# Second mixer of a three-part network: probabilities and values as rounded high and low parts, their product in three passes

## The chip, the core and the metric

The kernel runs on one core of one Trainium2 chip. A core has a matrix engine (TensorE, PE in the profile; its weight loads are PEld), a vector engine (VectorE, DVE), an activation engine (ScalarE, ACT), a general engine (GpSimd, POOL) and a queue engine (SyncE, SP). The engines run beside each other, each takes its own instructions in their order, and they wait for each other by semaphores. The working memory (SBUF) has 128 partitions; TensorE writes into eight banks of 128x512 float32 numbers (PSUM). The metric is the device time of one execution in microseconds (us).

## The reference

A sequence of 512 rows of width 1024 goes through two layers of feed-forward parts and mixers and one hybrid layer. The change is in the mixer of the second layer, eight heads of differential attention:

```python
q = rms_norm(q.reshape(B, S, DIFF_HEADS, 2, DIFF_DH), qk_norm_g[0]) * (DIFF_DH ** -0.5)
k = rms_norm(k.reshape(B, S, DIFF_HEADS, 2, DIFF_DH), qk_norm_g[1])
p1 = jax.nn.softmax(jnp.einsum('bhqd,bhkd->bhqk', q1b, k1) + bias, axis=-1)
p2 = jax.nn.softmax(jnp.einsum('bhqd,bhkd->bhqk', q2b, k2) + bias, axis=-1)
return jnp.einsum('bhqk,bhkv->bhqv', p1 - lam * p2, vh)
...
out = rms_norm(out, subln_g) * (1.0 - lam_init)
return out.reshape(B, S, DIFF_V).astype(h.dtype) @ w_out
```

The last einsum of the attention is the product that the change touches: for each head 512 queries, 512 keys, 128 columns of values.

## The kernel before

Seven stages follow each other: ffn 0, gla (first mixer), ffn 1, ffn 2, diff (second mixer), ffn 3, hybrid. Weights arrive in panels by SyncE's queue. For each unit of 128 columns ScalarE writes a rounded high part (whi, type float32r) and VectorE the rest as a low part (wlo); TensorE then makes each product of a weight and an activation as three passes of rounded operands: high by high, high by low, low by high (rows, L1989).

In the second mixer the order of everything is one list, diff_steps (L231), and each engine's program walks through it and does its own part of each step. Head h has four query tiles n = 4h to 4h+3. The steps:

- half: four of the eight row tiles of one projection (k, q or v of one head), 12 passes on TensorE. With the second half VectorE subtracts a coming weight unit (w_lo) and multiplies the result out of PSUM (L1725 for q and k, L1720 for v).
- ss, rs, qk, hi, lo: norm of q and k. TensorE sums the squares, ScalarE takes the root, VectorE scales, ScalarE copies the rounded high parts (seven copies of half tiles: dif_k, dif_q), VectorE subtracts for the low parts (four, L1746).
- attend n: TensorE makes two score tiles of two passes each; VectorE adds the bias and takes the maximum (L1758, "the two maxima"); ScalarE takes the exponential.
- comb n: VectorE scales and joins the two tiles into the probabilities (L1787 to L1793).
- turn n: TensorE transposes the four 128x128 blocks of the probabilities into bank 5 (L1986), ScalarE copies the bank to DPT, shown as dif_pt.
- vT h: TensorE transposes the values into bank 6, ScalarE copies them to DV, shown as dif_v.
- pv h: TensorE multiplies DV and DPT, four plain float32 products (L2387), into bank 7.
- oss, o, y: norm of the head's output; begin and more: parts of the output projection, begun while the last head is still going.

In the middle of the stage the list of one pass of its loop (h = 2 to 5) is this; h = 1 begins at half q, and h = 6 ends at half v:

```
half k0, vT h, attend n, comb n-1, o h-2, half k1, turn n-2, half q0,
attend n+1, comb n, turn n-1, half q1, attend n+2, comb n+1, pv h-1, ss h+1,
half v0, rs, qk, hi h+1, turn n, attend n+3, comb n+2, half v1, lo h+1,
oss h-1, turn n+1
```

Turn n waited for d_pt, the copy of turn n-1, because both use bank 5. The product pv waited for the copies of its head's values and of its four turns. ScalarE's order is that of the list too: the copy of turn n comes after hi h+1. All matmuls stand under L1982, all transposes under L1986, and all of ScalarE's instructions under L771 or L772, the lines of the helpers.

Of the kernel before, what the change touches and what calls it, by code (L numbers as in the profile page):

```python
# [9 lines left out]
ALU = mybir.AluOpType  # L10
# [41 lines left out]
NCOLS = _n  # L52
STAGE = 21792

# [347 lines left out]
d_hi_q d_hi_k d_lo_q d_lo_k d_v d_vT d_vrow  # L402
d_score d_max d_exp d_comb d_turn d_pt d_pv d_osq d_oss d_y d_yhi d_ylo
gs h_z h_hi h_conv0 h_conv h_gmm h_gates h_ri h_ix h_tanh h_a h_ln h_m h_sqrt h_one h_b h_scan
# [5 lines left out]
def build(nc, a):  # L410
    with ExitStack() as ctx:
# [74 lines left out]
        with ExitStack() as mem:  # L486
            def t_(name, shape, dt=F32):
                return sb("dif_" + name, shape, dt, mem)

            O = t_("y", [128, 8, S])  # L490
            bt = [t_(f"bias{i}", [128, 896]) for i in range(2)]
            qb = [t_(f"qb{i}", [128, S]) for i in range(2)]
            dsq = [t_(f"sq{i}", [128, S]) for i in range(2)]
            drq = [t_(f"rq{i}", [128, S]) for i in range(2)]
            dparts = [[t_(f"{n}{i}", [128, S], F32R) for n in ("q0", "q1", "k0", "k1", "kl0", "kl1")] for i in range(2)]
            dvt = t_("vt", [128, S])
            DV = [t_(f"v{i}", [128, 4, 128]) for i in range(2)]
            dpb = [[t_(f"p{i}{j}", [128, S]) for j in range(2)] for i in range(3)]
            DPT = t_("pt", [128, 4, S])
            dst = [t_(f"st{i}", [128, 8]) for i in range(3)]  # L500
# [812 lines left out]
        def dve_program(e):  # L1313
# [390 lines left out]
            def diff():  # L1704
                u = first["diff"]
                zero_halves(dparts)
                for s in DS:
                    if s[0] == "half":
                        _, tag, h, half = s
# [54 lines left out]
                    elif s[0] == "o":  # L1764
                        h = s[1]
                        w.wait_ge(sem["lnb"], rsqrt_done(("d_o", h)))
                        e.scalar_tensor_tensor(out=O[:, h, :], in0=psum[DIF_PV][:, :], scalar=lam[:, 7:8], in1=sqs[:, :],
                                               op0=ALU.mult, op1=ALU.mult).then_inc(sem["d_y"], 1)
                    elif s[0] == "y":
                        n = s[1]  # L1770
                        w.wait_ge(sem["d_yhi"], n + 1)
                        e.tensor_tensor(xl[:, n, :], O[:, n, :], xh[:, n, :].bitcast(F32),
                                        ALU.subtract).then_inc(sem["d_ylo"], 1)
                    elif s[0] == "begin" and s[1]:
                        w_lo(u)

            def zero_halves(parts):
# [200 lines left out]
        def pe_program(e):  # L1978
# [332 lines left out]
            def diff_misc_free(key):  # L2311
# [5 lines left out]
                elif key[0] == "vT":  # L2317
                    w.wait_ge(sem["d_vrow"], key[1] + 1)
                else:
                    w.wait_ge(sem["lnb"], ln_done(("q", key[1])))  # L2320

            def diff():
                u = first["diff"]
                misc, in_free, got = None, [], {}
                for s in DS:
# [48 lines left out]
                    elif s[0] == "turn":  # L2374
                        n = s[1]
                        w.wait_ge(sem["d_comb"], 4 * n + 4)
                        if n:
                            w.wait_ge(sem["d_pt"], n)
                        turned(DIF_TURN, dpb[n % 3][0], 4, sem["d_turn"])
                    elif s[0] == "pv":  # L2380
                        h = s[1]
                        w.wait_ge(sem["d_vrow"], h + 1)
                        w.wait_ge(sem["d_pt"], 4 * h + 4)
                        if h:
                            w.wait_ge(sem["d_y"], h)
                        for c in range(4):
                            ins = mm(psum[DIF_PV][:, :], DV[h % 2][:, c, :], DPT[:, c, :], c == 0, c == 3)  # L2387
                        ins.then_inc(sem["d_pv"], 1)
# [21 lines left out]
            def out_bank_free(m):  # L2410
# [7 lines left out]
                elif m == 5:  # L2418
                    w.wait_ge(sem["d_pt"], 32)
                elif m == 6:  # L2420
# [345 lines left out]
```

## Time and profile before

| | |
|---|---|
| median of 3 runs | 2163.85 us (2163.83 to 2165.5) |
| profiled execution | 2163.63 us, of which the span is 2161.8 |
| busy, share of the span | TensorE 99%, weight loads 85%, VectorE 78%, ScalarE 54%, GpSimd 12% |
| chain that ended last | TensorE 91%, VectorE 4%, ScalarE 2% |
| product of the second mixer | 64 records from 1365.8 to 1547.1 us |

Busy shares are means over all stages. What one stage waits for is read from the stage itself: in the rows in order of time, a bracket gives the idle time of an engine ahead of an instruction and what released it. The records of matmuls overlap, so their distance from start to start is what each costs, not their length.

### The profile page before, as it was taken

How to read it: one execution, taken by the hardware profiler on the slowest of the kernel's cores; microseconds unless marked ns; L12 is line 12 of the kernel's file. 1: busy time of each engine (PE TensorE's matmuls, PEld its weight loads, DVE VectorE, ACT ScalarE, POOL GpSimd, SP SyncE). 2: the span in 40 equal slices, each digit the busy share in tenths (PEclk: the TensorE clock that was granted, in tenths of full speed). 3: DMA queues.
4: the chain of work that ended last, by engine and by line, in shares of the span. 5: the costliest groups of instructions: out<-in, count | busy, mean ns of one | idle time of the engine just before them, and what ended most of it. 6: DMA issues, size and time to landing. Idle time of an engine off the chain costs nothing.

```text
span 2161.8 us, 33546 instructions
## 1 busy us (share of the span) xinstructions
PE 2144.5 (99%) x13412; PEld 1835.3 (85%) x13412; DVE 1680.9 (78%) x2546; ACT 1176.7 (54%) x1922; POOL 253.0 (12%) x187
## 2 busy tenths in 40 slices
PE   9999999999999999999999999999999999999999
PEld 6989897777779898989899997777789898977777
DVE  8789697988678796888787787777688886966873
ACT  6536264667556263546355356777555362638672
POOL 3000004000040000040010112000130000030000
PEclk9999999999999999999999999999999999999999
DMA  7454535131135555354554542222135545332211
GB/s 214 123 136 99 151 94 161 40 98 60 46 89 141 124 137 151 84 162 125 176 129 127 122 126 92 77 75 95 50 79 150 137 100 150 98 131 74 79 59 39
DMA packets 249451, 237.75 MB, mean 110 GB/s; under 512 B 4984, under 2 KB 245240, under 8 KB 249296
## 3 DMA queue, kind: packets, MB, share of 16 engines
q1 hardware_dynamic: 208336, 210.25, 30.3%
q0 software_dynamic: 40752, 25.11, 8.7%
q8 instruction: 107, 1.75, 0.3%
q14 instruction: 48, 0.39, 0.1%
q10 hardware_dynamic: 208, 0.24, 0.0%
HBM read 213.79 MB, written 6.32 MB: 102 GB/s over the span
## 4 chain that ended last, share of the span: by engine, by line
PE 91%; DVE 4%; ACT 2%; issue 1%; DMA 0%; SPq 0%; ACTq 0%; DVEq 0%
PE ps L1982 90%; PE ps L1986 1%; DVE sb_wlo L1334 1%; DMA sb_raw<-ffn_w_gu 0%; ACT sb_whi L771 0%; DVE sb_gla_ek L1689 0%; DVE sb_gla_eq L1692 0%; ACT sb_hyb_th L771 0%; ACT sb_lnb L771 0%; DVE sb_gla_cf L1681 0%; DVE sb_gla_xb L1684 0%; DVE sb_gla_d L1669 0%; SPq L737 0%; DVE sb_rb L1965 0%; ACT sb_xh L771 0%
## 5 line engine op out<-in xcount | busy, mean ns | idle before, releaser
L1982 PE MATMUL ps<-sb_xh,sb_whi 128*128 128x512 f32 (+1 forms) x1812 | 625.4, 345 | 3.6 <-issue 1.8
L1982 PE MATMUL ps<-sb_xl,sb_whi 128*128 128x512 f32 (+1 forms) x1812 | 608.8, 337 | 0.1
L1982 PE MATMUL ps<-sb_xh,sb_wlo 128*128 128x512 f32 (+1 forms) x1812 | 606.7, 337 | 0.0
L771 ACT ACTIVATE sb_whi<-sb_raw 128x1024 fp32r<-128x1024 f32 (+1 forms) x368 | 379.9, 1037 | 376.6 <-PE ps L1982 359.8
L1982 PEld LDWEIGHTS ps<-sb_xh,sb_whi 128*128 128x128 f32 x1812 | 344.0, 190 | 56.8 <-issue 20.4
L1982 PEld LDWEIGHTS ps<-sb_xl,sb_whi 128*128 128x128 f32 x1812 | 344.2, 190 | 39.3 <-DVE sb_xl L1354 3.3
L1982 PEld LDWEIGHTS ps<-sb_xh,sb_wlo 128*128 128x128 f32 x1812 | 343.9, 190 | 37.1
L1982 PE MATMUL ps<-sb_ffn_tl,sb_whi 128*128 128x256 f32 x1200 | 339.6, 283 | 0.0
L1982 PE MATMUL ps<-sb_ffn_th,sb_whi 128*128 128x256 f32 x1200 | 339.6, 283 | 0.0
L1982 PE MATMUL ps<-sb_ffn_th,sb_wlo 128*128 128x256 f32 x1200 | 339.6, 283 | 0.0
L1334 DVE TENSOR_TENSOR sb_wlo<-sb_raw,sb_whi 128x1024 fp32r<-128x1024 f32 (+1 forms) x218 | 275.6, 1271 | 49.1 <-ACT sb_whi L771 48.6
L1982 PE MATMUL ps<-sb_ffn_ah,sb_whi 128*128 128x512 f32 x704 | 275.4, 391 | 0.0
L1982 PE MATMUL ps<-sb_ffn_ah,sb_wlo 128*128 128x512 f32 x704 | 274.1, 389 | 0.0
L1982 PE MATMUL ps<-sb_ffn_al,sb_whi 128*128 128x512 f32 x704 | 274.1, 389 | 0.0
L1982 PEld LDWEIGHTS ps<-sb_ffn_tl,sb_whi 128*128 128x128 f32 x1200 | 230.4, 192 | 0.0
L1982 PEld LDWEIGHTS ps<-sb_ffn_th,sb_wlo 128*128 128x128 f32 x1200 | 230.4, 192 | 0.0
L1982 PEld LDWEIGHTS ps<-sb_ffn_th,sb_whi 128*128 128x128 f32 x1200 | 230.4, 192 | 0.0
L2600 POOL DMA_DIRECT2D sb_raw<-sb_raw x75 | 96.4, 1350 | 989.5 <-DMA sb_raw<-ffn_w_gu 736.2
L1327 DVE TENSOR_TENSOR sb_wlo<-sb_raw,sb_whi 128x1024 fp32r<-128x1024 f32 x150 | 182.7, 1218 | 2.4 <-ACT sb_whi L771 2.4
L771 ACT ACTIVATE sb_whi<-sb_ffn_sums 128x1024 fp32r<-128x1024 f32 (+1 forms) x150 | 125.7, 841 | 83.4 <-DVE sb_ffn_sums L1349 64.5
L1982 PEld LDWEIGHTS ps<-sb_ffn_ah,sb_wlo 128*128 128x128 f32 x704 | 132.1, 188 | 27.9
L1982 PEld LDWEIGHTS ps<-sb_ffn_ah,sb_whi 128*128 128x128 f32 x704 | 132.2, 188 | 26.9
(293 smaller groups left out, 2919.9 us busy)
## 6 DMA issues: line engine op xcount, KB each, us to landing
sb_raw<-ffn_w_gu SPq DMA_DIRECT2D x86, 1024.0 KB, 5.8
sb_raw<-ffn_w_down SPq DMA_DIRECT2D x32, 1024.0 KB, 5.1
sb_raw<-sb_raw POOLq DMA_DIRECT2D x75, 256.0 KB, 4.2
sb_raw<-w_ada SPq DMA_DIRECT2D x12, 1024.0 KB, 7.6
sb_raw<-ffn_w_down SPq DMA_DIRECT2D x16, 768.0 KB, 5.6
sb_raw<-gla_w_in SPq DMA_DIRECT2D x12, 1024.0 KB, 5.5
sb_raw<-diff_w_in SPq DMA_DIRECT2D x12, 1024.0 KB, 5.1
sb_raw<-w_in SPq DMA_DIRECT2D x10, 1024.0 KB, 5.1
```

The lines of the kernel that those rows point to most:

```text
L771: return e.activation(out, in_, func, bias=bias, scale=scale)
L1327: e.tensor_tensor(lo, fast_source(u), hi.bitcast(F32), ALU.subtract).then_inc(sem["w_lo"], 1)
L1334: e.tensor_tensor(lo, raw[panel % NRAW][:, 0:nk, off:off + 128], hi.bitcast(F32), ALU.subtract).then_inc(sem["w_lo"], 1)
L1982: return e.matmul(out, lhsT, rhs, start=start, stop=stop, skip_group_check=skip)
L1986: ins = e.transpose(psum[bank][:, c * 128:(c + 1) * 128], src[:, c * 128:(c + 1) * 128], ident)
L2600: e.dma_start(raw[up % NRAW][:, 0:4, off:off + 128], raw[gate % NRAW][:, 0:4, off:off + 128], accum_op=ALU.add).then_inc(sem[f"s_pre{i % 2 ...
```

## The change

The probabilities and the values of the second mixer are kept as two rounded parts. ScalarE's copies out of banks 5 and 6 now write the rounded high part (type float32r), and VectorE subtracts it from the same bank for the low part (new tiles DPTL and DVL). The product of a head becomes 12 passes: for each of four tiles high by high, high by low and low by high. The next turn, the next use of bank 6 after a vT, and the product now wait for the subtraction (d_ptl, d_vlo). VectorE does a subtraction after its next step that has work for it, or when the next turn or vT comes in the list. The first half of a projection has no VectorE work and is skipped in this. The two new tiles take 12 KB per partition; the stages' memory grows by that, and the build reserves less for dynamic DMAs.

```diff
-STAGE = 21792
+STAGE = 24864
...
-            DV = [t_(f"v{i}", [128, 4, 128]) for i in range(2)]
+            DV, DVL = ([t_(f"{n}{i}", [128, 4, 128], F32R) for i in range(2)] for n in ("v", "vl"))
...
-            DPT = t_("pt", [128, 4, S])
+            DPT, DPTL = t_("pt", [128, 4, S], F32R), t_("ptl", [128, 4, S], F32R)
...
             def diff():
                 u = first["diff"]
                 zero_halves(dparts)
+                turned_last = None
                 for s in DS:
+                    if s[0] in ("turn", "vT"):
+                        if turned_last is not None:
+                            low_of_turned(*turned_last)
+                        turned_last = s
+                        if s == ("turn", 31):
+                            low_of_turned(*turned_last)
+                            turned_last = None
+                        continue
                     if s[0] == "half":
                         _, tag, h, half = s
                         if not half:
                             continue
...
                     elif s[0] == "begin" and s[1]:
                         w_lo(u)
+                    else:
+                        continue
+                    if turned_last is not None:
+                        low_of_turned(*turned_last)
+                        turned_last = None
+
+            def low_of_turned(kind, n):
+
+                if kind == "turn":
+                    w.wait_ge(sem["d_pt"], n + 1)
+                    if n >= 4:
+                        w.wait_ge(sem["d_pv"], n // 4)
+                    out = slice(n % 4 * 128, n % 4 * 128 + 128)
+                    e.tensor_tensor(DPTL[:, :, out], psum[DIF_TURN][:, :].rearrange("p (c q) -> p c q", q=128),
+                                    DPT[:, :, out].bitcast(F32), ALU.subtract).then_inc(sem["d_ptl"], 1)
+                else:
+                    w.wait_ge(sem["d_vrow"], n + 1)
+                    if n >= 2:
+                        w.wait_ge(sem["d_pv"], n - 1)
+                    e.tensor_tensor(DVL[n % 2][:, :, :], psum[DIF_MISC][:, :].rearrange("p (s c) -> p s c", c=128),
+                                    DV[n % 2][:, :, :].bitcast(F32), ALU.subtract).then_inc(sem["d_vlo"], 1)
...
                 elif key[0] == "vT":
-                    w.wait_ge(sem["d_vrow"], key[1] + 1)
+                    w.wait_ge(sem["d_vlo"], key[1] + 1)
...
                         w.wait_ge(sem["d_comb"], 4 * n + 4)
                         if n:
-                            w.wait_ge(sem["d_pt"], n)
+                            w.wait_ge(sem["d_ptl"], n)
                         turned(DIF_TURN, dpb[n % 3][0], 4, sem["d_turn"])
                     elif s[0] == "pv":
                         h = s[1]
-                        w.wait_ge(sem["d_vrow"], h + 1)
-                        w.wait_ge(sem["d_pt"], 4 * h + 4)
+                        w.wait_ge(sem["d_vlo"], h + 1)
+                        w.wait_ge(sem["d_ptl"], 4 * h + 4)
                         if h:
                             w.wait_ge(sem["d_y"], h)
                         for c in range(4):
-                            ins = mm(psum[DIF_PV][:, :], DV[h % 2][:, c, :], DPT[:, c, :], c == 0, c == 3)
+                            mm(psum[DIF_PV][:, :], DV[h % 2][:, c, :], DPT[:, c, :], c == 0, False)
+                            mm(psum[DIF_PV][:, :], DV[h % 2][:, c, :], DPTL[:, c, :], False, False)
+                            ins = mm(psum[DIF_PV][:, :], DVL[h % 2][:, c, :], DPT[:, c, :], False, c == 3)
...
-    nc = bacc.Bacc("TRN2", target_bir_lowering=False, num_devices=1)
+    nc = bacc.Bacc("TRN2", target_bir_lowering=False, num_devices=1, dynamic_dma_scratch_size=4096)
```

## Rows read from the trace of the kernel before

**Rows 1.** The page: busy time by engine; the chain that ended last, by engine.
```profile
PE 2144.5 (99%) x13412; PEld 1835.3 (85%) x13412; DVE 1680.9 (78%) x2546; ACT 1176.7 (54%) x1922; POOL 253.0 (12%) x187
...
PE 91%; DVE 4%; ACT 2%; issue 1%; DMA 0%; SPq 0%; ACTq 0%; DVEq 0%
```

**Rows 2.** Groups by form, 1300 to 1570 us: busy, mean ns, idle before.
```profile
L1982 PE MATMUL ps<-sb_dif_pt,sb_dif_v 128*128 128x512 f32 x64 | 28.8, 592 | 0.0
...
L1725 DVE TENSOR_TENSOR sb_dif_qb<-ps,sb_rb 128x512 f32<-128x512 f32 x16 | 10.9, 683 | 1.0 <-ACT sb_rb L771 1.0
```

**Rows 3.** Order of time, TensorE around pv 2: start, length, engine, instruction.
```profile
1420.72 0.39 PE L1982 MATMUL ps<-sb_dif_k,sb_dif_q 128*128 128x512 f32 x1
...
1421.63 3.59 PE L1982 MATMUL ps<-sb_dif_pt,sb_dif_v 128*128 128x512 f32 x8
1425.15 1.09 PE L1982 MATMUL ps<-sb_dif_sq,sb_cst 64*64 64x512 f32 x8
```

**Rows 4.** Order of time, around attend 13 and turn 11.
```profile
1416.79 0.57 ACT L771 ACTIVATE sb_dif_pt<-ps 128x512 f32<-128x512 f32 x1
...
1417.25 0.69 DVE L1758 CUSTOM_DVE_ANT_0 sb_dif_p<-ps,sb_dif_bias 128x512 f32<-128x512 f32 x1 [1.69 <-PE ps L1982]
...
1417.51 0.63 PE L1986 MATMUL ps<-sb_cst,sb_dif_p 128*128 128x128 f32 x4
...
1418.48 0.16 DVE L1787 RECIPROCAL sb_dif_st<-sb_dif_st 128x2 f32<-128x2 f32 x1
```

**Rows 5.** Order of time, end of the half projection of q ahead of pv 2.
```profile
1420.49 0.39 PE L1982 MATMUL ps<-sb_xh,sb_wlo 128*128 128x512 f32 x1
...
1421.07 0.68 DVE L1725 TENSOR_TENSOR sb_dif_qb<-ps,sb_rb 128x512 f32<-128x512 f32 x1
```

**Rows 6.** Order of time, from attend 15 to attend 16.
```profile
1431.38 0.16 DVE L1787 RECIPROCAL sb_dif_st<-sb_dif_st 128x2 f32<-128x2 f32 x1
...
1432.83 1.22 DVE L1334 TENSOR_TENSOR sb_wlo<-sb_raw,sb_whi 128x1024 fp32r<-128x1024 f32 x1
...
1433.25 0.60 ACT L771 ACTIVATE sb_dif_pt<-ps 128x512 f32<-128x512 f32 x1
...
1436.00 1.40 DVE L1746 TENSOR_TENSOR sb_dif_q<-sb_dif_qb,sb_dif_q 64x512 fp32r<-64x512 f32 x2
...
1437.59 0.48 PE L1982 MATMUL ps<-sb_dif_k,sb_dif_q 128*128 128x512 f32 x1
```

**Rows 7.** Order of time, from attend 27 to attend 28.
```profile
1515.21 1.40 DVE L1746 TENSOR_TENSOR sb_dif_kl<-sb_dif_qb,sb_dif_k 64x512 fp32r<-64x512 f32 x2
...
1516.65 1.40 DVE L1746 TENSOR_TENSOR sb_dif_q<-sb_dif_qb,sb_dif_q 64x512 fp32r<-64x512 f32 x2
1517.08 0.60 ACT L771 ACTIVATE sb_dif_pt<-ps 128x512 f32<-128x512 f32 x1
...
1517.83 0.63 PE L1986 MATMUL ps<-sb_cst,sb_dif_p 128*128 128x128 f32 x4 [0.66 <-ACT sb_dif_pt L771]
...
1518.75 0.80 PE L1982 MATMUL ps<-sb_dif_k,sb_dif_q 128*128 128x512 f32 x1
```

**Rows 8.** Order of time, the last head: attend 28, a wait, pv 6, attend 30, turn 31.
```profile
1521.60 0.68 DVE L1758 CUSTOM_DVE_ANT_0 sb_dif_p<-ps,sb_dif_bias 128x512 f32<-128x512 f32 x1
...
1524.47 0.69 DVE L1772 TENSOR_TENSOR sb_xl<-sb_dif_y,sb_xh 128x512 fp32r<-128x512 f32 x1 [1.57 <-ACT sb_xh L771]
...
1531.49 3.59 PE L1982 MATMUL ps<-sb_dif_pt,sb_dif_v 128*128 128x512 f32 x8
...
1533.53 0.68 DVE L1758 CUSTOM_DVE_ANT_0 sb_dif_p<-ps,sb_dif_bias 128x512 f32<-128x512 f32 x1
...
1540.88 0.63 PE L1986 MATMUL ps<-sb_cst,sb_dif_p 128*128 128x128 f32 x4
```

**Rows 9.** Busy us in a window, then granted clock (1.00 is full), DMA share, GB/s.
```profile
1400.00:1450.00 50.00, 50.00 (x231) 37.89 (x230) 39.01 (x83) 38.16 (x73) 1.07 (x2) 1.00 0.26 82
```

**Rows 10.** DMA issues by line: size of one, median us from issue to landing.
```profile
sb_raw<-sb_raw POOLq DMA_DIRECT2D x75, 256.0 KB, 4.2
```

More of the change, by code:

```diff
@@ L402 @@
 d_hi_q d_hi_k d_lo_q d_lo_k d_v d_vT d_vrow
-d_score d_max d_exp d_comb d_turn d_pt d_pv d_osq d_oss d_y d_yhi d_ylo
+d_score d_max d_exp d_comb d_turn d_pt d_ptl d_vlo d_pv d_osq d_oss d_y d_yhi d_ylo
 gs h_z h_hi h_conv0 h_conv h_gmm h_gates h_ri h_ix h_tanh h_a h_ln h_m h_sqrt h_one h_b h_scan
@@ L2418, in out_bank_free @@
                 elif m == 5:
-                    w.wait_ge(sem["d_pt"], 32)
+                    w.wait_ge(sem["d_ptl"], 32)
                 elif m == 6:
```

## The prediction

> **What bounds the kernel now.** I read the page first: busy time by engine and the chain that ended last [rows 1]. TensorE is busy for 99% of the span and makes 91% of the chain, so a microsecond of TensorE work that goes away can be a microsecond gained, and every wait put in front of TensorE costs its full length. Then the groups by form between 1300 and 1570 us, the second mixer with its edges [rows 2]: the product of probabilities and values is one of its groups, and the VectorE form that the new subtractions would have is another. Last the stage in order of time, engine by engine, at the places where the changed waits sit [rows 3 to 8]. TensorE takes its instructions strictly in the written order, VectorE and ScalarE too. So for each new wait I asked which instruction of VectorE releases it and what stands ahead of that one. The sum is made against the profiled execution, 2163.63 us, of which 2161.8 is the span; that is 0.22 below the median of the three runs, 2163.85, and I add the same number to either. One head is h, its four query tiles are n = 4h to 4h+3, and low(n) is the new subtraction behind turn n.
>
> **The product itself.** One head's product is 8 records, four plain 128x512 products in two records each, and the next instruction begins 1425.15 - 1421.63 = 3.52 us after it [rows 3], 0.88 us each. The three passes have the form of the scores, 128x512 with rounded operands, of which four take 1421.63 - 1420.72 = 0.91, 0.2275 each [rows 3]. Twelve of them take 12 x 0.2275 = 2.73. The gain is 0.79 per head, 6.3 over eight heads. Since scores of this form are in the trace I take no other value. Writing rounded values from ScalarE's copies should cost nothing: it already writes this type elsewhere at the same size.
>
> **The low parts.** 32 + 8 subtractions of 128x512, one operand in PSUM. The nearest row is the multiplication at L1725, 0.683 us [rows 2], and VectorE begins the next instruction some 0.07 before one ends: two maxima of 0.69 take 1418.48 - 1417.25 = 1.23 [rows 4]. So 0.61 each in a row and 0.68 to the end. 40 x 0.61 = 24 us of VectorE work. If all of it fell into VectorE's idle time it would cost nothing; if all lay on the path, 24 us. Neither end decides, because the waits do. I go through one regular head, h = 3.
>
> Wait A, turn n-1 behind low(n-2). In the written order VectorE does low(n-2) only after the two maxima of attend n+1, and TensorE comes to turn n-1 directly after the scores of attend n+1. Before, that turn needed only ScalarE's copy, which had begun at 1416.79, and started at 1417.51. The maxima begin at 1417.25 and are through at 1418.48 [rows 4]. There low(10) begins, which turn 11 now needs; it ends at 1418.48 + 0.68 = 1419.16, and with a tenth for the hand-over the turn starts at 1419.26: 1.75 late, six times (h = 1 to 6). No slack elsewhere can hide it, since the maxima need the very scores that TensorE has just done. Waiting behind that turn are the next half projection and all of TensorE's queue.
>
> Wait B, pv behind low(n-1). This one stands behind the half projection of q and its multiplication on VectorE. The last pass of that half began at 1420.49, ended 0.39 later, and shifts by 1.75 to 1422.63. VectorE needs 1421.07 - 1418.48 = 2.59 for a combination and a weight subtraction, so from 1419.09 it is ready at 1421.68 and the multiplication begins at 1422.68 [rows 4, 5]. low(n-1) follows at 1423.29, ends at 1423.97, and pv starts at 1424.03. TensorE would be there at 1421.63 + 1.75 = 1423.38 [rows 3]. So 0.65, six times (pv 0 to 5).
>
> Wait C, VectorE itself. low(n) stands directly after the maxima of attend n+3, which end at 1431.38. It needs ScalarE's copy of turn n, and ScalarE does that one after the seven copies of high parts of the next k and q, from 1433.25 to 1433.85 [rows 6]. VectorE thus stands still for 2.47 us, then works 0.61. Queued behind it are a combination (1432.83 - 1431.38 = 1.45), a weight subtraction, v's multiplication and the four subtractions at L1746, the last of which ended at 1436.00 + 1.40 = 1437.40; TensorE's attend of the next head needs them and started at 1437.59. That slack is 0.19, of which 0.1 is hand-over. New end 1437.40 + 2.47 + 0.61 = 1440.5, scores at 1440.6: 3.0 late, five times (ahead of attend 8, 12, 16, 20, 24). A shorter wait of TensorE for low(n) at turn n+1 lies inside it. The trace shows the cause already once without the change: at 1517.83 TensorE waited 0.66 for such a copy [rows 7].
>
> Hidden: low(n+1) follows those subtractions and runs while TensorE does the first two score passes (0.46, and 0.39 to the end of a record); the values' low part goes into the 1.69 us in which VectorE waited ahead of attend n+1 [rows 4]. If that cover were gone they would cost 0.61 each per head. At h = 0 I take nothing, and 3 x 0.61 = 1.8 as the upper bound.
>
> A regular head is 1.75 + 0.65 + 3.0 - 0.79 = 4.6, five of them 23.1. Head 6 up to its ss: 1.75 + 0.65 - 0.79 = 1.6.
>
> The tail (from turn 24). VectorE is ready at 1515.21, waits for the copy that ends at 1517.68, and the four subtractions then end at 1521.2 rather than 1518.05; attend 28, written at 1518.75 [rows 7], slips to 1521.3. Four more VectorE instructions of 0.61 (v's multiplication, three of y) and the maxima of attend 28 begin at 1523.6 rather than 1521.60. From there to the first maximum of attend 30 VectorE took 11.93, of which 1.57 was a wait for ScalarE that is now over in time [rows 8]; with four low parts of 0.61 (25, the values, 26, 27) it is 12.8, so low(27) ends at 1536.4. pv 6 needs it: 1536.5 rather than 1531.49. It ends at 1539.2, turn 28 (0.35) and attend 31 follow, its maxima begin 0.75 behind its first pass and end at 1541.5, low(28) 0.61, two combinations 2.9, low(29) 0.68 and the hand-over, turn 30 at 1545.8, its copy 1547.0, low(30) 1547.7, turn 31 at 1547.8 rather than 1540.88: 6.9 late. pv 7 keeps its distance to turn 31 and gives back 0.79: 6.1. pv 6's own gain is swallowed, as VectorE sets the pace there.
>
> Sum: 23.1 + 1.6 + 6.1 = 30.8. **Forecast 2163.63 + 30.8 = 2194.4 us**, some 1.4% slower. The stage behind starts that much later and is otherwise unchanged.
>
> The smaller DMA scratch. The build now reserves 4096 bytes per partition for the dynamic DMAs where nothing was said before. The DMAs that GpSimd issues in software are in question, above all 75 gate additions of 256 KB, 4.2 us to landing each [rows 10]. I take zero, since the same descriptors are issued in the same order; as the far bound I let a quarter of each landing time more come onto the path, 75 x 1 = 75 us. The Trainium skill (SBUF — State Buffer, section "SBUF size: 192, 224, or 256?") says of that scratch that it is the descriptor ring of these DMAs; it says nothing of what a smaller one does, and no row here shows it.
>
> **Rivals.** First, VectorE's stall C is absorbed. For it: VectorE was busy for only 39.01 of 50 us in a window of this stage [rows 9]. Against: hardly any of that idle time lies between the stall and the scores that wait for it [rows 6]. It gives 6 x (1.75 + 0.65 - 0.79) + 6.1 = 15.8: 2179.4 us. Second, on the other side: the low parts are hidden and only the passes count. Its place is turn n-1: it decides once the low part of turn n-2 ends before TensorE leaves attend n+1, so if VectorE could take it before the maxima, in the 1.69 us that it sits idle ahead of them [rows 4], in all six heads. Then -6.3: 2157.3 us. Against it stands the written order. Third, TensorE's clock. The granted clock is 1.00, which is 2.4 GHz, in a window in which TensorE is busy for all 50 us [rows 9]; now it idles for up to 3 us a time. If after each of the five stalls C twelve passes (2.75 us) ran at 1.2 in place of 2.4 GHz, that is 5 x 2.75 = 13.8 more: 2208. The Trainium skill (TensorE: Matmul & The Clock Gate, the table "Why this matters for your kernels") warns that gaps between bursts throw the clock to half, and by that rule this change would pay twice for its longest waits; no gap of such length in this stage of the trace tests it. Fourth, the DMA scratch matters: the forecast plus up to 75.
>
> **How the numbers follow.** Forecast 0.72, C absorbed 0.14, clock 0.04, scratch 0.03, hidden and faster 0.04, stalls and gain about cancelling 0.03. The range 2177 to 2206 takes in the first two and an error of 2 us per head in C; it leaves out about 0.15. About 0.2% is what a measurement of this kernel tells from no change. Faster 0.04, same 0.03, slower 0.93.
>
> **What would show it.** In the profile after: twelve records per product at a 0.23 pitch; TensorE idle 1.75 ahead of six turns and 0.65 ahead of six products, released by the subtraction; VectorE idle 2.5 ahead of low(n), released by ScalarE's copy; TensorE idle some 2.5 to 3 ahead of the first scores of five heads, released by L1746; other stages unchanged to 0.5 us. A turn n-1 that starts without idle time would refute A, and a first score of a head within 0.5 us of its old distance would refute C.

## The result and the profile after

The changed kernel takes 2204.63 us (median of 4 runs, 2203.67 to 2206.82) against 2163.84 before. The ratio is 1.0188, with a 95% interval of 1.017 to 1.0206. The profiled execution is the shortest of the four, 2203.67 us, with a span of 2201.9 us, 40.1 longer. The prediction said slower by 30.8, range 13 to 42. Executions of one kernel can lie steps of about 1.5 us apart, those of the kernel before too: the longer ones have a lower mean clock, and in five profiled ones of them (of kernels below) TensorE's clock fell for a moment in the first 100 us of the program (granted clock 0.98 there, otherwise 1.00).

The page of the changed kernel: busy time by engine, then the chain that ended last, to be set beside [rows 1].

```profile
PE 2151.2 (98%) x13444; PEld 1844.6 (84%) x13444; DVE 1706.7 (78%) x2586; ACT 1179.7 (54%) x1922; POOL 253.4 (12%) x187
...
PE 86%; DVE 7%; ACT 4%; issue 2%; DMA 0%; SPq 0%; DVEq 0%; ACTq 0%
```

TensorE's busy time is 6.7 us longer although its product is cheaper; that is the first hint of a slower clock, shown below. Its part of the chain fell from 91% to 86%, and VectorE's grew from 4% to 7% and ScalarE's from 2% to 4%.

Groups by form, 1300 to 1610 us, beside [rows 2]: busy us, mean ns of one, idle time of the engine ahead and its releaser. Matmuls now stand under L2012, transposes under L2016, the new subtractions under L1798 (turns) and L1804 (values).

```profile
L1798 DVE TENSOR_TENSOR sb_dif_ptl<-ps,sb_dif_pt 128x512 fp32r<-128x512 f32 x32 | 22.0, 687 | 17.8 <-ACT sb_dif_pt L771 17.7
...
L2016 PE MATMUL ps<-sb_cst,sb_dif_p 128*128 128x128 f32 x128 | 19.7, 276 | 16.6 <-DVE sb_dif_st L1817 12.8 <-DVE sb_dif_ptl L1798 3.8
...
L2012 PE MATMUL ps<-sb_dif_pt,sb_dif_v 128*128 128x512 f32 x32 | 13.3, 414 | 6.2 <-DVE sb_dif_ptl L1798 6.2
...
L2012 PE MATMUL ps<-sb_dif_ptl,sb_dif_v 128*128 128x512 f32 x32 | 12.5, 391 | 0.0
L2012 PE MATMUL ps<-sb_dif_pt,sb_dif_vl 128*128 128x512 f32 x32 | 12.5, 391 | 0.0
...
L1804 DVE TENSOR_TENSOR sb_dif_vl<-ps,sb_dif_v 128x512 fp32r<-128x512 f32 x8 | 5.5, 684 | 0.0
```

The idle column shows the new waits: TensorE 16.6 us ahead of turns (A and parts of C and of the tail) and 6.2 ahead of products (B, and 3.3 ahead of product 6), VectorE 17.8 ahead of its own new subtraction, mostly C. The values' subtraction never waited.

Order of time, wait A at attend 13 and turn 11 in the pass of head 3, then wait B at product 2 (start, length, instruction, idle ahead), beside [rows 4, 5, 3].

```profile
1430.25 0.69 DVE L1767 CUSTOM_DVE_ANT_0 sb_dif_p<-ps,sb_dif_bias 128x512 f32<-128x512 f32 x1 [2.46 <-PE ps L2012]
...
1431.48 0.69 DVE L1798 TENSOR_TENSOR sb_dif_ptl<-ps,sb_dif_pt 128x512 fp32r<-128x512 f32 x1
...
1432.31 0.63 PE L2016 MATMUL ps<-sb_cst,sb_dif_p 128*128 128x128 f32 x4 [1.65 <-DVE sb_dif_st L1817]
...
1435.72 0.69 DVE L1734 TENSOR_TENSOR sb_dif_qb<-ps,sb_rb 128x512 f32<-128x512 f32 x1 [0.97 <-PE ps L2012]
...
1436.33 0.68 DVE L1798 TENSOR_TENSOR sb_dif_ptl<-ps,sb_dif_pt 128x512 fp32r<-128x512 f32 x1
...
1437.06 0.50 PE L2012 MATMUL ps<-sb_dif_pt,sb_dif_v 128*128 128x512 f32 x1 [0.47 <-DVE sb_dif_ptl L1798]
...
1440.01 1.09 PE L2012 MATMUL ps<-sb_dif_sq,sb_cst 64*64 64x512 f32 x8
```

VectorE takes the two maxima (from 1430.25), then the low part of turn 10 (1431.48, ended 1432.17), and the turn starts 0.14 later. The profile names L1817 as the releaser, a small instruction that began at 1432.08; the subtraction ended last of the things that this turn's code waits for. B is the same picture behind q's multiplication.

Order of time, wait C (ScalarE's copy of turn 12, VectorE, TensorE's first score of attend 16), beside [rows 6].

```profile
1446.80 1.28 ACT L771 ACTIVATE sb_dif_q<-sb_dif_qb 64x512 fp32r<-64x512 f32 x2
1448.11 0.60 ACT L771 ACTIVATE sb_dif_pt<-ps 128x512 fp32r<-128x512 f32 x1
...
1448.74 0.69 DVE L1798 TENSOR_TENSOR sb_dif_ptl<-ps,sb_dif_pt 128x512 fp32r<-128x512 f32 x1 [2.43 <-ACT sb_dif_pt L771]
...
1453.96 1.40 DVE L1755 TENSOR_TENSOR sb_dif_q<-sb_dif_qb,sb_dif_q 64x512 fp32r<-64x512 f32 x2
...
1455.42 0.50 PE L2012 MATMUL ps<-sb_dif_k,sb_dif_q 128*128 128x512 f32 x1 [2.01 <-DVE sb_dif_q L1755]
```

TensorE behind the same wait one head earlier, and three windows (columns as in [rows 9]: busy us of TensorE, weight loads, VectorE, ScalarE and GpSimd, then the granted clock).

```profile
1421.04 0.50 PE L2012 MATMUL ps<-sb_dif_k,sb_dif_q 128*128 128x512 f32 x1 [2.01 <-DVE sb_dif_q L1755]
1421.38 0.39 PE L2012 MATMUL ps<-sb_dif_kl,sb_dif_q 128*128 128x512 f32 x1
1421.61 0.57 PE L2012 MATMUL ps<-sb_dif_k,sb_dif_q 128*128 128x512 f32 x1
1421.97 0.63 PE L2012 MATMUL ps<-sb_dif_kl,sb_dif_q 128*128 128x512 f32 x1
1422.40 0.63 PE L2012 MATMUL ps<-sb_xh,sb_whi 128*128 128x512 f32 x1
...
1424.53 0.63 PE L2012 MATMUL ps<-sb_xh,sb_wlo 128*128 128x512 f32 x1
1424.96 0.45 PE L2012 MATMUL ps<-sb_xh,sb_whi 128*128 128x512 f32 x1
1425.25 0.39 PE L2012 MATMUL ps<-sb_xl,sb_whi 128*128 128x512 f32 x1
```

```profile
1500.00:1550.00 50.00, 43.51 (x202) 32.24 (x202) 35.36 (x78) 33.59 (x63) 0.54 (x1) 1.00 0.24 77
...
1418.00:1426.00 8.00, 5.99 (x22) 4.53 (x21) 7.58 (x17) 2.78 (x6) 0.00 (x0) 0.79 0.00 0
1421.97:1425.00 3.03, 3.03 (x9) 2.34 (x8) 2.83 (x9) 1.63 (x4) 0.00 (x0) 0.50 0.00 0
```

Seven passes stand 0.43 us apart in place of 0.23: for 3 us the granted clock was 0.50, the lower level of 1.2 GHz. I call this a fall of the clock. It came behind four of the five C waits. From 1500 to 1550, around the fifth, the clock stayed at 1.00 although TensorE was busy for only 43.51 of 50 us. From product to product a head with a fall takes 34.38 us, the fifth, without one, 32.80; so each fall costs 1.57.

The last head, beside [rows 8].

```profile
1553.79 0.50 PE L2012 MATMUL ps<-sb_dif_k,sb_dif_q 128*128 128x512 f32 x1 [1.17 <-DVE sb_dif_q L1755]
...
1558.98 0.69 DVE L1781 TENSOR_TENSOR sb_xl<-sb_dif_y,sb_xh 128x512 fp32r<-128x512 f32 x1 [0.89 <-ACT sb_xh L771]
...
1569.97 0.50 PE L2012 MATMUL ps<-sb_dif_pt,sb_dif_v 128*128 128x512 f32 x1 [3.32 <-DVE sb_dif_ptl L1798]
```

The ledger of the span, each term as a distance between the same two instructions in both traces, taken where no fall of the clock lies in between:

| term | predicted | measured |
|---|---|---|
| A, first score of attend n to turn n-1, six times | 1.75 | 9.69 - 7.86 = 1.83 |
| B, turn to product, six times | 0.65 | 4.75 - 4.12 = 0.63 |
| product, to the sum of squares behind it, six times | -0.79 | 2.95 - 3.52 = -0.57 |
| C, sum of squares to next first score, five times | 3.0 | 15.41 - 12.44 = 2.97 |
| product 7 and all behind it | -0.79 | 617.03 - 617.70 = -0.67 |
| clock behind C | none | 4 x 1.57 = 6.3 |
| last head, attend 27 to product 7 | 6.9 | 39.06 - 30.86 = 8.2 |

11.0 + 3.8 + 14.9 + 6.3 + 8.2, less 6 x 0.57 = 3.4 and 0.7, is 40.1 for 40.1 measured. The stage began at the same time as before (within 0.1 us), and nothing is left over for head 0 or the stages behind.

The bracket of a matmul shows less than the wait costs, because a pass is recorded as 0.39 long though the next one follows after 0.23. With these 0.16 added, B's recorded 0.47 becomes the 0.63 of the ledger and A's 1.65 becomes 1.81 of 1.83. C has two brackets, 2.01 ahead of the first score and 0.54 at turn n+1, and with 2 x 0.16 they make 2.87 of 2.97.

### The profile page after: what moved, and what is told of

It is laid out like the page before. It is cut to its first block, busy times and chain, and to the rows that moved or that the text cites. A ratio compares the mean times of both kernels' runs of the same rounds, so it can differ in the third digit from the quotient of the medians.

```text
span 2201.9 us, 33657 instructions
## 1 busy us (share of the span) xinstructions
PE 2151.2 (98%) x13444; PEld 1844.6 (84%) x13444; DVE 1706.7 (78%) x2586; ACT 1179.7 (54%) x1922; POOL 253.4 (12%) x187
## 3 DMA queue, kind: packets, MB, share of 16 engines
q8 instruction: 107, 1.75, 0.3%
## 4 chain that ended last, share of the span: by engine, by line
PE 86%; DVE 7%; ACT 4%; issue 2%; DMA 0%; SPq 0%; DVEq 0%; ACTq 0%
PE ps L2012 85%; DVE sb_wlo L1334 1%; PE ps L2016 1%; ACT sb_dif_k L771 1%; DVE sb_dif_ptl L1798 1%; ACT sb_whi L771 1%; DVE sb_dif_p L1767 1%; ACT sb_lnb L771 0%; DMA sb_raw<-ffn_w_gu 0%; DVE sb_dif_kl L1755 0%; DVE sb_dif_q L1755 0%; DVE sb_gla_ek L1689 0%; DVE sb_gla_eq L1692 0%; ACT sb_dif_q L771 0%; ACT sb_hyb_th L771 0%
## 5 line engine op out<-in xcount | busy, mean ns | idle before, releaser
L2012 PE MATMUL ps<-sb_xh,sb_whi 128*128 128x512 f32 (+1 forms) x1812 | 626.9, 346 | 3.1 <-issue 1.8
L2012 PE MATMUL ps<-sb_xl,sb_whi 128*128 128x512 f32 (+1 forms) x1812 | 610.6, 338 | 0.6 <-DVE sb_xl L1354 0.5
L2012 PE MATMUL ps<-sb_xh,sb_wlo 128*128 128x512 f32 (+1 forms) x1812 | 608.2, 338 | 0.0
L2012 PEld LDWEIGHTS ps<-sb_xh,sb_whi 128*128 128x128 f32 x1812 | 345.4, 191 | 57.1 <-issue 20.2
L2012 PEld LDWEIGHTS ps<-sb_xl,sb_whi 128*128 128x128 f32 x1812 | 345.6, 191 | 39.8 <-DVE sb_xl L1354 3.5
L2012 PEld LDWEIGHTS ps<-sb_xh,sb_wlo 128*128 128x128 f32 x1812 | 345.0, 190 | 37.6
L2012 PE MATMUL ps<-sb_ffn_th,sb_whi 128*128 128x256 f32 x1200 | 339.6, 283 | 0.0
L2012 PE MATMUL ps<-sb_ffn_tl,sb_whi 128*128 128x256 f32 x1200 | 339.6, 283 | 0.0
L2012 PE MATMUL ps<-sb_ffn_th,sb_wlo 128*128 128x256 f32 x1200 | 339.6, 283 | 0.0
L2012 PE MATMUL ps<-sb_ffn_ah,sb_whi 128*128 128x512 f32 x704 | 275.4, 391 | 0.0
L2012 PE MATMUL ps<-sb_ffn_ah,sb_wlo 128*128 128x512 f32 x704 | 274.1, 389 | 0.0
L2012 PE MATMUL ps<-sb_ffn_al,sb_whi 128*128 128x512 f32 x704 | 274.1, 389 | 0.0
L2012 PEld LDWEIGHTS ps<-sb_ffn_th,sb_whi 128*128 128x128 f32 x1200 | 230.4, 192 | 0.0
L2012 PEld LDWEIGHTS ps<-sb_ffn_tl,sb_whi 128*128 128x128 f32 x1200 | 230.4, 192 | 0.0
L2012 PEld LDWEIGHTS ps<-sb_ffn_th,sb_wlo 128*128 128x128 f32 x1200 | 230.4, 192 | 0.0
L2012 PEld LDWEIGHTS ps<-sb_ffn_ah,sb_wlo 128*128 128x128 f32 x704 | 132.1, 188 | 28.0
L2012 PEld LDWEIGHTS ps<-sb_ffn_al,sb_whi 128*128 128x128 f32 x704 | 132.3, 188 | 26.7
```

The source lines that it names most:

```text
L2012: return e.matmul(out, lhsT, rhs, start=start, stop=stop, skip_group_check=skip)
```

## The experiments

**The passes alone.** The kernel before with rounded tiles and twelve passes, without low parts.

```diff
-                            ins = mm(psum[DIF_PV][:, :], DV[h % 2][:, c, :], DPT[:, c, :], c == 0, c == 3)
+                            mm(psum[DIF_PV][:, :], DV[h % 2][:, c, :], DPT[:, c, :], c == 0, False)
+                            mm(psum[DIF_PV][:, :], DV[h % 2][:, c, :], DPT[:, c, :], False, False)
+                            ins = mm(psum[DIF_PV][:, :], DV[h % 2][:, c, :], DPT[:, c, :], False, c == 3)
```

> The kernel before with ScalarE's copies rounded and the product as twelve rounded passes, but no low parts and none of their waits: high by high stands in all three places, so the low parts are left out of the result. Theory (the waits cost all of it): one product takes 11 x 0.2285 + 0.32 = 2.83 us rather than 3.52, as in the changed kernel's trace, so 8 x 0.69 = 5.5 faster: 2158.3 us, with no new idle time of TensorE over 0.3 us. Rival (the passes or the rounded copies themselves cost time): no faster than 2163.8, up to 2204.

Measured 2158.38 us, 0.9975 (0.9965 to 0.9984). Product to product 27.22 us, before 27.94: 0.72 per head. That is the change's gain if nothing waits, 5.4 us (5.5 had been expected). TensorE has no idle time in the heads between product 0 and product 5.

**The scratch alone**, the kernel before with the one argument `dynamic_dma_scratch_size=4096`.

> The kernel before with the smaller scratch for dynamic DMAs alone. Theory: nothing, 2163.8 us within 0.1%, and the gate additions land in 4.2 us as before. Rival (the ring costs part of the 10 us by which the forecast fell short): 2168 to 2174 us, and a longer time to landing.

Measured 2163.81 against 2163.80 of the kernel before beside it (0.9991 to 1.001), and the 75 gate additions landed 4.2 us after their issue, as in [rows 10]. The fourth rival is out.

**The waits alone.** The changed kernel with the four plain products.

```diff
-                            mm(psum[DIF_PV][:, :], DV[h % 2][:, c, :], DPT[:, c, :], c == 0, False)
...
+                            ins = mm(psum[DIF_PV][:, :], DV[h % 2][:, c, :].bitcast(F32),
+                                     DPT[:, c, :].bitcast(F32), c == 0, c == 3)
```

> The changed kernel with its low parts and all its waits, but the product as four plain float32 products of the high parts; the low parts are computed and waited for, and left out of the result. Theory (waits cost, passes gain): the loss stays and the gain goes, 2204.6 + 7 x 0.57 + 0.7 = 2209.3 us. Rival (the twelve passes bring part of the loss): below 2204.

Measured 2208.66, 1.0208 (1.0187 to 1.0228), with the same waits (1.65, 0.47, 2.01). Heads without a fall of the clock take 33.4 to 33.5 in place of 32.8, and a plain product behind a wait takes 3.63 (2.95 for the twelve passes). So the passes still gain 0.68 per product while the waits stay. The medians are only 4.0 apart, for the clock fell three times in the stage here (behind two of the five C waits and behind the 3.35 us ahead of product 6) and four times in the changed kernel: 4.1 us between the profiled spans and one fall of 1.6 make 5.7. The expected 2209.3 was close in part by luck, for it counted neither this nor the 0.68. There are only two executions of this kernel.

**The idle time filled.** Nine passes whose result is overwritten stand ahead of the first score of heads 2 to 6, where TensorE waited 2.01.

```diff
+                        if n % 4 == 0 and 8 <= n <= 24:
+                            w.wait_ge(sem["d_max"], 2 * n - 2)
+                            for _ in range(9):
+                                mm(psum[DIF_RING[2 * n % 3]][:, :], xh[:, 0, 0:128], xh[:, 0, :], True, True)
```

> The changed kernel with nine more passes of 0.2275 us, 2.05 in sum, ahead of the first scores of attend 8, 12, 16, 20 and 24, written into the bank that the first score overwrites: work for TensorE just where it waits 2.01 us for VectorE. Theory (the halved clock behind those waits costs 4 x 1.57 us): the granted clock stays 1.00 and the time falls by 6.3 to 2198.3 us although work was added. Rival (the clock falls for another reason, the pace of the whole stage): the clock falls as before, 2204 to 2206 us. If the filling is too long, up to 5 x 0.2 us more in either case.

Measured 2199.82, 1.0167 (1.0152 to 1.0182). All five heads take 32.8 us, none 34.4, though TensorE has more to do: the falls need the idle time. Of the 6.3 us 4.8 came back. In the profiled execution the clock fell once behind the 3.34 us wait ahead of product 6, which the changed kernel's profiled one did not have.

**A undone by order.** For n = 4, 8 to 24, the first line in VectorE's list of steps, the others in ScalarE's:

```diff
+        put(("turn", n - 2), ("half", "k", n // 4 + 1, 1), 1)
...
+        out.remove(("turn", n - 2))
+        out.insert(out.index(("half", "k", n // 4 + 1, 1)), ("turn", n - 2))
```

> Wait A alone undone: ScalarE copies bank 5 for turn n-2 ahead of its squares of half k1, and VectorE takes the low part of turn n-2 directly behind half k1, in the idle time ahead of the maxima of attend n+1, for n = 4, 8 to 24. Everything is computed as in the changed kernel. My theory, that the waits add up and each depends on its own place in VectorE's order: the recorded 1.65 us of TensorE ahead of each of the six turns n-1 is gone, the distance from the first score of attend n+1 to the turn goes back from 9.69 to about 7.9, B (0.47) and C (2.01) stay at their lengths, and so do the falls of the clock behind C. Six times 1.84 is 11.0: 2204.6 - 11.0 = 2193.6 us. Rival, that the waits hide each other (a stall taken away at A only makes VectorE later at B or C): less than 4 us gained, 2201 to 2204. Rival, that the clock falls because of A and C together: also 6.3 more gained, 2187.

Measured 2192.22, 1.013 (1.0116 to 1.0144): 12.4 less, for 11.0 expected. The profiled spans are 11.3 apart: six times 1.65, and one fall of the clock less (two behind C in place of four, but one behind product 6's wait); together 11.5. Of the kernel with A undone, TensorE in heads 2 and 3:

```profile
1399.60 0.50 PE L2038 MATMUL ps<-sb_dif_pt,sb_dif_v 128*128 128x512 f32 x1 [0.65 <-DVE sb_dif_ptl L1824]
1412.16 0.63 PE L2042 MATMUL ps<-sb_cst,sb_dif_p 128*128 128x128 f32 x4 [0.57 <-DVE sb_dif_st L1843]
1418.00 0.50 PE L2038 MATMUL ps<-sb_dif_k,sb_dif_q 128*128 128x512 f32 x1 [2.01 <-DVE sb_dif_q L1786]
1430.76 0.50 PE L2038 MATMUL ps<-sb_dif_pt,sb_dif_v 128*128 128x512 f32 x1 [0.61 <-DVE sb_dif_ptl L1824]
```

No turn n-1 waits any more (turn 11, at 1425.86, has no idle time ahead of it; the 0.57 ahead of the turn at 1412.16 is C's second wait, at turn n+1). C kept its 2.01. B has grown from 0.47 to some 0.64, against the expectation. A head is down from 32.80 to 31.15, by 1.65: A's 1.83 less 0.17 at B. So the waits add up but for a tenth, and the rival of mutual hiding falls.

**C undone by order.** The first two lines are VectorE's, for the heads 1 to 5 (n = 4 to 20); the last is ScalarE's, with h = n/4 + 1, and it also moves the copy of turn 24:

```diff
+        put(("turn", n), ("comb", n + 2), 1)
+        out.insert(out.index(("half", "v", n // 4 + 1, 0)), ("wlo",))
...
+        out[i:i + 1] = [("hi", h, "k"), ("turn", n), ("hi", h, "q")]
```

> Wait C alone undone: ScalarE copies bank 5 for turn n between the high parts of k and those of q, VectorE takes the low part of turn n behind the combination n+2 in place of directly behind the maxima of attend n+3, and the weight subtraction of half v1 stands ahead of half v0, for the heads 1 to 5. Everything is computed as in the changed kernel. My theory: the distance from ss to the first score of the next head falls from 15.41 to 12.4 to 12.9 (12.44 before the change); TensorE's recorded 2.01 us there becomes under 0.5, and with it all four falls of the clock in this stretch go (6.3 us). A and B stay: six times 1.65 and 0.47 recorded. 2204.6 - 5 x (2.5 to 3.0) - 6.3 = 2183 to 2186 us. Rival, that the clock falls because of A: then 2190 to 2192. Rival, that VectorE has too little time for the added subtractions in a head, whatever their order: C only moves, and no more than 5 us come back, 2199 or more.

Measured 2183.35, 1.0087 (1.0072 to 1.0103). All six waits A are there with 1.65, the 2.01 are gone from every head, and a head takes 29.80: 27.94 + 1.83 + 0.63 - 0.57 is 29.83, so C is gone completely. The clock fell behind none of these heads, only once behind the 3.35 us ahead of product 6. A alone thus causes no fall, and with A undone two still came behind C.

**A, B and C undone, the tail left**, and **the same with the tail's low parts reordered.** B's edit and the tail's:

```diff
+        put(("turn", n - 1), ("half", "q", n // 4 + 1, 1), 0)
...
+    out[i:i + 2] = [("lo", 7, "k"), ("low", ("turn", 24)), ("lo", 7, "q")]
+    put(("turn", 27), ("begin", 1, 4), 0)
+    put(("turn", 29), ("comb", 31), 0)
+    put(("turn", 30), ("comb", 31), 1)
```

> A, B and C undone in the heads 1 to 6 by order alone, the tail left as in the changed kernel; all is computed. It splits the tail's loss into order and amount. If the tail's 8.2 us is mostly order (the low parts placed where VectorE or TensorE wait), this kernel loses 3 to 5 us against the one with the tail reordered too: 2165.6 to 2167.6 us, and TensorE again waits over 3 us ahead of the product of head 6 with one fall of the clock behind it (1.6). If it is amount alone, the two are within 1 us: 2162.6 to 2163.6.

> A, B and C undone together by order alone, and the low parts of the tail (turns 24, 27, 29, 30) put ahead of or between steps at which VectorE stood idle. Everything is computed as in the changed kernel: same passes, same 40 subtractions. My theory, that the loss is one of order and not of the amount of VectorE work: no wait above 0.5 us left ahead of turns and products up to head 6, clock 1.00 throughout, and the time near that of the kernel in which the passes were changed and the low parts left out (2158.4), plus about 1 to 2 us in the last two turns, whose low parts nothing can hide: 2159 to 2161 us, faster than the kernel before (2163.8). Rival, that 24 us more of VectorE work cost something anywhere they are put: 2168 or more, with VectorE busy and TensorE waiting for it in the middle of each head.

Measured 2168.1, 1.002 (1.0011 to 1.003), without the tail's edit and 2162.6, 0.9994 (0.9985 to 1.0003), with it. In both the middle heads take 27.2 to 27.3 us, as with the passes alone (27.22), with no idle time of TensorE recorded between product 0 and product 5, although VectorE makes all its 24 us of subtractions. In the middle the loss was order alone. The first kernel kept the 3.35 us ahead of product 6 and a fall of the clock behind it, and the medians are 5.5 apart (3 to 5 had been expected). From the first score of attend 27 to product 7 the changed kernel takes 39.06, this one 39.47 with the fall and 37.9 without it (ScalarE's copy of turn 24 stands earlier here too), the reordered one 34.62 and the kernel with the passes alone 30.49. So of the tail's loss 4.4 us were order, and a fall comes on top where the long wait stays. The reordered one missed its expectation of 2159 to 2161: from the stage's first sum of squares to product 7 it takes 220.82, the passes alone 216.54. Of the 4.3 between them 4.1 lie in the tail. Of the reordered kernel, the window 1521.7 to 1541 us:

```profile
1521.70:1541.00 19.30, 15.91 (x72) 11.52 (x73) 18.66 (x44) 10.24 (x23) 0.00 (x0) 1.00 0.17 56
```

VectorE is busy for 18.66 of 19.30 us. Seven low parts (the values of head 7, turns 25 to 30) at 0.61 are 4.3, near the 4.1. That alone is no proof; the next two kernels are the test.

**Is it VectorE's amount of work there?** Two kernels take work off that stretch. In the first the low part of the values goes behind that of turn 30, with the sum of squares of head 6 behind turn 31, and one weight subtraction (1.17) from begin 1 to begin 3; in the second the weight subtraction alone is moved.

```diff
-                    elif s[0] == "begin" and s[1]:
-                        w_lo(u)
+                    elif s[0] == "begin" and s[1] in (1, 3):
+                        w_lo(u - (s[1] == 1))
```

> The kernel with A, B, C and the tail reordered (2162.6 us) still loses 4.6 us of span against the kernel with the passes alone, and its trace shows no idle time of TensorE up to turn 24; from 1521.7 us to the end of the low part of turn 30 VectorE has no gap, and its seven low parts there (values of head 7, turns 25 to 30) are 7 x 0.61 = 4.3 us. My theory: in the tail alone it is the amount of VectorE work that counts. This kernel takes two pieces of work off that stretch and changes nothing else of what is computed: the low part of the values of head 7 goes behind that of turn 30 (with the sum of squares of head 6 on TensorE behind turn 31), and of the two weight subtractions at begin 1 the second goes to begin 3. 0.61 + 1.17 = 1.8 less: turn 31 starts 1.8 earlier, 2160.8 us. Rival, that VectorE is not the bound there but the chain of copies by ScalarE between the turns: under 0.5 gained, 2162.1 to 2162.6. Rival, that the moved pieces are only late somewhere else (TensorE waits at begin 3 or at the product of head 7): 2162 or more.

> The kernel with everything reordered (2162.6 us) and one edit more: of the two weight subtractions of begin 1 the second goes to begin 3, where VectorE has time; TensorE's list is unchanged and GpSimd does none of it. My theory, that VectorE's amount of work bounds the stretch from 1521.7 us to turn 31 and that the gain of the earlier trial (turn 31 1.68 earlier, product of head 7 only 0.68) was lost to the work moved behind turn 31: here turn 31 and the product of head 7 both come about 1.17 earlier, 2161.4 us. Rival, that what follows turn 31 is bound by something else (ScalarE's root and the o of head 6): turn 31 1.17 earlier, the product not: 2162.3 to 2162.6.

Measured 2163.4, 0.9997 (0.9988 to 1.0006), and 2161.92, 0.9991 (0.9982 to 1.0), for 2160.8 and 2161.4 expected. In the first of the two most executions have the early fall of the clock, and both profiled ones have it, so I compare inside the stage. (Without it the first takes 2161.9 to 2162.1: it missed its expectation all the same.) From its first sum of squares, turn 31 starts at 217.59 in the reordered kernel, 215.93 and 216.49 here: 1.66 and 1.10 earlier for 1.78 and 1.17 us of work taken away. VectorE's amount of work is thus the bound up to turn 31. Product 7 follows only 0.66 earlier in the first and 1.12 in the second: the first had moved TensorE's own work (the sum of squares of head 6) behind turn 31, where TensorE has no idle time to put it in. The second is the best version found that computes the same. Its executions without that early fall take 2161.4 to 2161.9 and those of the kernel before, beside them, 2163.6 to 2164.0: some 2.2 us less, 0.1%.

**GpSimd takes both weight subtractions of begin 1**, and begin 3 stands ahead of turn 31.

```diff
+                for u in (first_out["diff"] + 2, first_out["diff"] + 3):
...
+                    e.tensor_tensor(wlo[u % NSLOT][:, 0:nk, :], raw[panel % NRAW][:, 0:nk, off:off + 128],
+                                    whi[u % NSLOT][:, 0:nk, :].bitcast(F32), ALU.subtract).then_inc(sem["w_lo"], 1)
```

> In the kernel with everything reordered TensorE still stood idle for 0.25 + 0.61 + 1.62 + 0.65 = 3.1 us between turns 27 and 31, behind a VectorE without a gap; taking 1.78 us off VectorE there brought turn 31 1.68 earlier, but the product of head 7 only 0.68, because work of TensorE had been moved behind turn 31. Here the two weight subtractions of begin 1 (2.35 us of VectorE, 1528.24 to 1530.51) are done by GpSimd, which had nothing to do between 1486 and 1558 us, and the six passes of begin 3 (1.4 us) stand ahead of turn 31 in place of behind the product of head 7; the sum of squares of head 6 and the low part of the values stay where they were. All is computed. My theory, that the tail's rest is VectorE's amount of work: turn 31 about 2.3 us earlier less what begin 3 takes of TensorE there beyond the idle time, the product of head 7 and what follows 2 to 3.1 earlier: 2159.5 to 2160.6 us, 0.998 of the kernel before. Rival, that GpSimd's reads and writes beside VectorE slow VectorE down by as much as they save: its instructions of 0.48 to 0.75 us in that stretch get longer, 2162 or more.

Measured 2163.1, 0.9995 (0.9986 to 1.0004), for 2159.5 to 2160.6 expected: a miss, for two reasons. Of this kernel, GpSimd and VectorE:

```profile
1508.91 2.65 POOL L2719 TENSOR_TENSOR sb_wlo<-sb_raw,sb_whi 128x1024 fp32r<-128x1024 f32 x1 [21.96 <-ACT sb_whi L824]
...
1510.04 2.07 DVE L1797 SCALAR_TENSOR_TENSOR sb_dif_qb<-sb_dif_qb,sb_par,sb_dif_rq 128x512 f32<-128x512 f32 x1 [0.74 <-ACT sb_dif_rq L824]
...
1524.44 2.41 POOL L2719 TENSOR_TENSOR sb_wlo<-sb_raw,sb_whi 128x1024 fp32r<-128x1024 f32 x1 [12.89 <-ACT sb_whi L824]
...
1525.21 0.69 DVE L1853 TENSOR_TENSOR sb_dif_vl<-ps,sb_dif_v 128x512 fp32r<-128x512 f32 x1
...
1526.01 0.86 DVE L1869 TENSOR_TENSOR sb_dif_st<-sb_dif_st,sb_small 128x1 f32<-128x1 f32 x1
```

The two long VectorE instructions (1510.04 and 1526.01) took 0.75 and 0.16 in the reordered kernel: 1.3 and 0.7 lost, and TensorE's wait ahead of turn 25 grew from 0.76 to 1.36. So the rival had part of the truth. Second, with begin 3 ahead of it TensorE had no gap before turn 31, which started 217.69 after the first sum of squares, no earlier than in the reordered kernel (217.59), and product 7 (at 221.26) now waited 0.2 for the o of head 6.

## Why the prediction was right, and where it was off

**Wait A**: confirmed, 1.83 for 1.75, six times, and undoing the order alone takes it away.

**Wait B**: confirmed, 0.63 for 0.65.

**Wait C**: confirmed, 2.97 for 3.0, and VectorE's wait 2.43 for 2.47. The cause named, ScalarE's copy behind the copies of the high parts, is what the profile names as the releaser of VectorE's wait. The kernel that moves this copy lost the wait, and with it all of C; it moves the low part and a weight subtraction too, so the copy's own share is not shown apart. Of the signs one was off: TensorE's idle time ahead of the first scores was to be 2.5 to 3 and is 2.01, since 0.54 of it stands at turn n+1.

**Hidden low parts**: confirmed. The ledger leaves nothing over for them or for head 0, and the heads with A, B and C undone take no longer than with the passes alone.

**The product itself**: the step failed in size. The pitch of 0.23 is right, but a product behind a wait starts more slowly (1437.06 to 1437.40, 0.34 to the second pass), and 0.32 pass between the last pass and the sum of squares. So 0.57 in place of 0.79, 0.2 less per product. Half of that is no property of the passes, for a plain product behind the same wait is slower too, 3.63 in place of 3.52; like with like the gain is 0.68, and 0.72 per head with no wait ahead.

**The clock**: the rival that the text gave 0.04. It happened, not alone but on top of the forecast, at 6.3 us in place of the 13.8 it was priced at: four falls of 1.57, where five of 2.75 had been worked out. The step that failed was to treat it as another case rather than as a possible cost of each long wait which the forecast itself had put in. With 6.3 the forecast would have been 2200.7.

**The range**: 2204.6 lies inside 2177 to 2206 partly by luck. Its upper part was there for an error of 2 us per head in C, which did not come: C was right to 0.03. What filled it was the clock (6.3), the smaller gain of the passes (1.5) and the tail (1.3), none of which the range had been made for.

**The tail**: 8.2 in place of 6.9. The shifts of attend 28 (2.5) and its maxima (2.0) came as worked out. But the step "a wait for ScalarE that is now over in time" failed: VectorE still waited 0.89 of the 1.57 at the fourth y (1558.98). ScalarE was late itself; that it was so by the same cause is likely, but no run takes it apart. Turn 31 then came 2.3 later behind product 6 rather than 1.9.

**Scratch** at zero: confirmed. **C absorbed** and **hidden and faster** did not happen in this order; the second came about in the middle heads once the order was changed, as its condition said (the low part of turn n-2 in VectorE's idle time ahead of the maxima), though not with its 6.3 us: the last head takes back most of the gain.

What stays open is which wait the clock answers with a fall. Of the waits of 2.0 us, in the three kernels that had them unfilled, 8 of 15 were followed by one (4, 2 and 2 of 5, not in the same heads each time); of six waits of 3.3 us five; of 24 of 1.65 us none. I found nothing else in these traces that tells them apart.

## What to carry to other kernels

A new step on a shared engine costs what stands ahead of it in that engine's order. Here the same 24 us of VectorE work made the kernel 42 us longer (2204.6 against 2162.6) when its pieces, and the copies that release them, stood in the written order than when they were moved; 6 of the 42 are falls of the clock. Moved, they were free in the middle heads. In a stretch where the engine has no gaps left, as in the last head, order does not help and only the amount counts. Where a change adds long waits of TensorE (here from 2.0 us on), price a fall of its clock with each.

## What the runs showed of the hardware

Behind 8 of 15 idle times of 2.0 us TensorE's clock was down at 1.2 GHz for some seven passes of 128x512 (about 1.6 us lost each time); with the same time filled by passes it stayed at 1.00 in all five heads. The Trainium skill (TensorE: Matmul & The Clock Gate, the table "Why this matters for your kernels") advises against gaps between bursts of matmuls, but names longer ones than these. The direction agrees; on the length the measurement decides.

A subtraction of 128x1024 by GpSimd took 2.41 to 2.65 us (1.17 on VectorE) and held up VectorE where that read two operands from SBUF: the instruction begun at 1510.04 ended 0.55 after GpSimd's, the one begun at 1526.01 0.02 after it, while one that read a bank and one SBUF operand beside it (1525.21) kept its 0.69. The Trainium skill (SBUF — State Buffer, section "Who interferes with whom") says that the second SBUF input of such a VectorE instruction comes through a read interface that it shares with GpSimd, and that the shared ports are held exclusively. Both rows agree in the main: VectorE's instruction ends only after GpSimd's, though sooner behind it than by its usual 0.75 and 0.16 (GpSimd's spans are rough).
